# All low parts of the split weights made by VectorE, none by GpSimd

## The chip, the cores and the metric

The kernel runs on one core of one Trainium2 chip, as one launch. The metric is device time in microseconds (us), from the first instruction to the last, with what the launch puts around them. Lower is better. Engines are named as in the profile: PE is TensorE (PEld its weight load), DVE is VectorE, ACT is ScalarE, POOL is GpSimd, SP is the engine that issues the weight DMAs. L905 is line 905 of the kernel.

## The reference

256 tokens of width 1024 go through two stacks of two layers each, all in fp32. The first stack has four token mixers side by side in each layer (retention, a state-space scan, mLSTM, gated linear attention), a gated merge of their outputs, and a feed-forward: a plain one in layer 0, eight experts with top 2 in layer 1. The second stack has a modulation from a vector `c`, sliding-window attention and a feed-forward. Cut to what this change concerns, each mixer layer of the first stack is:

```python
def token_mixers(h, pos, w_in, ..., w_branch, w_out):
    u = h @ w_in                                   # 1024 -> all inputs of the four branches, and mgate (4096 columns)
    (rq, rk, rv, rg, sz, sxbc, sdt, gq, gk, gv, gr, ga,
     mqk, mv, mo, mi, mf, mgate) = _split_cols(u)
    ...                                            # four scans over the tokens, one per branch
    ybr = jnp.stack([y_ret, y_ssd, y_gla, y_ml], axis=2)
    gates = jax.nn.sigmoid(mgate.reshape(bsz, seq, N_BRANCH, D_MODEL))
    merged = jnp.sum(gates * jnp.einsum('bsnv,nvd->bsnd', ybr, w_branch), axis=2)
    return merged @ w_out
```

## The kernel before

**Split products.** A product in fp32 precision is made of three products of a faster format (fp32r). Each operand is written as a high part plus a low part, and TensorE adds high x high, high x low and low x high. The weights come from memory in pieces of 128 x 2048 numbers (1 MB), in a ring `raw` of 5 slots. For each piece, ScalarE makes the high part into `whi` (`split_high`, L899), and then one engine makes the low part into `wlo` as `raw - whi` (`split_low`, L905). `whi` and `wlo` have 3 slots each: ScalarE may write a slot only when TensorE has read the piece that was in it. SP loads a new piece into a slot of `raw` when the low part of the old one is made. The modulation weights (`ada_w`) are used in plain fp32 straight from `raw` and are not split at all.

**Which engine makes the low part.** `piece(name, of, lo_on)` takes `"V"` (VectorE) or `"G"` (GpSimd). `project_tokens` and `two_features` pass it on. In the kernel before, 24 pieces of each mixer layer, 48 in all, are marked `"G"`: retention's values (p0.2, two pieces), the middle piece of the state-space inputs (p1.1), mLSTM's values (p2.2, two), the gated attention's queries and values (p3.0, one, and p3.1, two), and the gates (g0.0 to g3.1, eight steps of two pieces). All other pieces are on VectorE.

**The order on each engine.** Each engine runs a list of steps. The order of the steps of a mixer layer is written out by hand in `MIXER`; steps such as `ret1`, `ssd4`, `gla5` are pieces of the scans and stand between the projections, so that TensorE has products to do while the vector work of a scan runs. Every step runs on TensorE, ScalarE and VectorE, each doing its own share of it. The splits are not in the list. They are put in by `wait_ge` and `split`: TensorE notes at each piece that it will need the two pieces after it as well (`AHEAD`), and when another engine is about to wait for a result of TensorE, it first makes its own share of all the pieces that TensorE had asked for by then:

```python
            if self.split_piece is not None and not self.splitting:
                self.reach = max(self.reach, self.board.need.get(key, 0))
                self.split()
```

So a low part on VectorE stands in the middle of the scan's vector work, at a place that this rule decides, and everything behind it on VectorE waits until its high part is there. A low part on GpSimd stands in a queue that holds little else: only the inverse roots of the norms (`inverse_root`, L1936 and L1938).

**Names in the rows.** L1460, L1466: small row operations of the mixers on 4 partitions (`rows3`, `rows4`). L568: the transposes `tokcol` that need them. L1359: taps of the causal convolution, with L1024 its tanh on ScalarE. L1496, L1498, L1500: rotary of the queries and keys (`ret1`), L491 and L492 the scores. L1383, L1384, L1035: decays of a scan. L1391, L1393, L1936, L1938, L1398: a head norm, over VectorE, GpSimd and VectorE again. L1413, L1417: merge of a gated branch. L1601 to L1605, L524, L1426: a level of the gated attention (`gla`): factors, scores, and the copy that frees the four PSUM banks of the level before. L410: any group of matmuls that add into one bank.

Of the kernel before, what the change touches and what calls it, by code (L numbers as in the profile page):

```python
# [14 lines left out]
P = 128  # L15
# [29 lines left out]
COLS = {}  # L45
# [131 lines left out]
def program(nc, a, out):  # L177
    with ExitStack() as ctx:
# [79 lines left out]
        rv, rg, rqk, rot_raw = carve(0, NT * MIX, NT * MIX, 4 * T, 4 * T)  # L258
        pad1, conv1, sz, xs, xdt = carve(1, 6 * (T + PAD), 6 * T, NT * MIX, NT * MIX, NT * MIX)
        mva, mo, pad2, conv2 = carve(2, NT * NH * (HD + 1), NT * MIX, 4 * (T + PAD), 4 * T)  # L260
        gv, gr, glaq, glak, glaG, glaE, glaX0, glaX1 = carve(3, NT * MIX, NT * MIX, *[T] * 6)
# [143 lines left out]
        def tensor_program(t):  # L405
# [62 lines left out]
            def two_features(name, w, c0, stage, lo_on="V"):  # L468
                read, parts = piece(name, full_piece(w, c0), lo_on)
                bank = t.take(name)  # L470
                for j in range(2):
                    m = project_features(full(parts), j * P, stage, bank, j * T)
                t.then_inc(m, ("full", name), read)
# [55 lines left out]
            def mixer_step(l, step):  # L529
                w, here = a["w_in"][l], (l, "mix")  # L530
                kind, _, n = step.partition(".")
                if step == "z":
                    read, parts = piece(("z", l), strips_piece(w, [(COLS[z], 32) for z in ("sdt", "ga", "mi", "mf")]))
                    bank = t.take(("z", l))
                    t.then_inc(project_features(full(parts, P), 0, here, bank, 0), ("full", ("z", l)), read)
                elif step == "alpha":
                    bank = t.take(("alpha", l))
                    t.wait_ge(("gate_feat", l))
                    at = COLUMN[("w_alpha", l)]
                    t.then_inc(group(bank[:, 0:T], [(cols[0:16, at:at + P], gate_feat[0:16, :])]), ("full", ("alpha", l)))  # L540
                elif step in ("p0.0", "p0.1"):
                    two_features(("p0", l, int(n)), w, COLS["rq" if n == "0" else "rk"], here)
                elif step == "p0.2":
                    project_tokens(("p0v", l), w, COLS["rv"], here, "G")
                elif kind == "p1" and n < "3":
                    two_features(("p1", l, int(n)), w, COLS["sxbc"] + int(n) * 2 * P, here, "G" if n == "1" else "V")
                elif step == "p1.3":
                    read, parts = piece(("p1z", l), full_piece(w, COLS["sz"]))
                    wf = full(parts)
                    for tt in range(NT):  # L550
                        bank = t.take(("p1z", l, tt))
                        m = product(bank[:, 0:MIX], [(stat_tokens(k, tt), (wf[0][:, k, :], wf[1][:, k, :])) for k in range(KD)])
                        t.then_inc(m, ("full", ("p1z", l, tt)), *([read] if tt else []))
                elif kind == "p2" and n < "2":
                    two_features(("p2", l, int(n)), w, COLS["mqk"] + int(n) * 2 * P, here)
                elif step == "p2.2":
                    project_tokens(("p2v", l), w, COLS["mv"], here, "G")
                elif step == "p3.0":
                    two_features(("p3", l), w, COLS["gq"], here, "G")
                elif step == "p3.1":  # L560
                    project_tokens(("p3v", l), w, COLS["gv"], here, "G")
                elif step == "tokcol":
                    t.wait_ge(("rows", l))
                    bank = t.take(("tokcol", l))
                    for i, r_ in enumerate((ACS, DT, CJ, TMP2)):
                        for tt in range(NT):
                            c = (i * NT + tt) * NH
                            m = transpose(bank[:, c:c + NH], row(r_)[:, pick_tokens(tt)], ident[0:NH, 0:NH])  # L568
                    t.then_inc(m, ("full", ("tokcol", l)))
                elif kind[0] == "d":  # L570
                    for z in mod_chunks["branch", 0][2 * int(kind[1:]):2 * int(kind[1:]) + 2]:
                        modulation_piece(*z)
                elif kind[0] == "g" and kind[1] != "l":
                    project_tokens(("g", l, int(kind[1]), int(n)), w, COLS["mgate"] + branch_order[int(kind[1])] * D + int(n) * BANK,
                                   here, "G")
                elif kind[0] == "a":
                    merge(l, int(kind[1]))
                elif kind[:3] == "ret":
                    retention(l, int(kind[3:]))
                elif kind[:3] == "ssd":  # L580
                    ssd(l, int(kind[3:]))
                elif kind[:2] == "ml":
                    mlstm(l, int(kind[2:]))
                elif kind[:3] == "gla":
                    gla(l, int(kind[3:]))
# [1603 lines left out]
```

## Time and profile before

| | us |
|---|---|
| time, median of 3 runs (lowest to highest) | 2478.57 (2476.72 to 2479.82) |
| the profiled execution, its time | 2476.41 |
| its span from first to last instruction | 2474.5 |
| PE busy in it | 2160.6 (87%) |
| DVE busy | 1543.9 (62%) |
| ACT busy | 1197.2 (48%) |
| POOL busy | 287.6 (12%) |

The profiled execution is 2.2 us below the median of the timed runs, and its time is 1.9 us longer than its span. Busy time is summed over an engine's instructions; matmuls overlap. An engine that is busy for 12% of the span can still hold up another one, so the table alone does not say what a change to it is worth. The two mixer layers of the first stack lie at about 20 to 400 us and 604 to 945 us; the experts of layer 1 follow until about 1800 us.

### The profile page before, as it was taken

How to read it: one execution, taken by the hardware profiler on the slowest of the kernel's cores; microseconds unless marked ns; L12 is line 12 of the kernel's file. 1: busy time of each engine (PE TensorE's matmuls, PEld its weight loads, DVE VectorE, ACT ScalarE, POOL GpSimd, SP SyncE). 2: the span in 40 equal slices, each digit the busy share in tenths (PEclk: the TensorE clock that was granted, in tenths of full speed). 3: DMA queues.
4: the chain of work that ended last, by engine and by line, in shares of the span. 5: the costliest groups of instructions: out<-in, count | busy, mean ns of one | idle time of the engine just before them, and what ended most of it. 6: DMA issues, size and time to landing. Idle time of an engine off the chain costs nothing.

```text
span 2474.5 us, 25557 instructions
## 1 busy us (share of the span) xinstructions
PE 2160.6 (87%) x10570; PEld 1769.1 (71%) x10570; DVE 1543.9 (62%) x1538; ACT 1197.2 (48%) x1251; POOL 287.6 (12%) x135
## 2 busy tenths in 40 slices
PE   6788778998889766999999999999967799787997
PEld 5676556886777654778787787877856488676886
DVE  2664454544456652788888888888855444554444
ACT  5443224443634322776676676766733344333442
POOL 2354400000337400000000000000000100100000
PEclk9888889998989888999999999999988799988999
DMA  8354556556434336799999999999961666523551
GB/s 260 103 190 168 187 191 235 189 184 193 135 119 153 119 117 237 263 353 330 341 345 339 360 325 338 366 341 345 362 219 59 230 205 197 189 85 96 189 189 54
DMA packets 369319, 550.49 MB, mean 222 GB/s; under 512 B 21030, under 2 KB 295078, under 8 KB 362150
## 3 DMA queue, kind: packets, MB, share of 16 engines
q1 hardware_dynamic: 365168, 534.82, 64.3%
q10 hardware_dynamic: 4028, 13.95, 1.5%
q8 instruction: 86, 1.41, 0.2%
q14 instruction: 37, 0.30, 0.0%
HBM read 547.58 MB, written 1.15 MB: 222 GB/s over the span
## 4 chain that ended last, share of the span: by engine, by line
PE 78%; DVE 10%; ACT 5%; DMA 2%; POOL 2%; issue 1%; ACTq 0%; SPq 0%; DVEq 0%; POOLq 0%
PE bank L410 74%; PE bank L436 2%; DVE wlo L905 2%; ACT whi L899 2%; POOL wlo L905 1%; DVE arena L1359 1%; POOL small L1938 1%; PE bank L485 1%; DVE arena L1500 1%; DMA raw<-in_moe_w 1%; DVE xn L1417 0%; DVE scoresB L1426 0%; ACT xn L964 0%; DVE arena L1498 0%; DMA xn<-in_lmask 0%
## 5 line engine op out<-in xcount | busy, mean ns | idle before, releaser
L905 DVE TENSOR_TENSOR wlo<-raw,whi 128x2048 fp32r<-128x2048 f32 (+1 forms) x413 | 944.2, 2290 | 403.7 <-ACT whi L899 403.6
L899 ACT ACTIVATE whi<-raw 128x2048 fp32r<-128x2048 f32 (+1 forms) x461 | 878.5, 1908 | 429.9 <-PE bank L410 374.1
L410 PE MATMUL bank<-whi,hThi 128*128 128x512 f32 (+2 forms) x1104 | 444.7, 403 | 41.5 <-POOL wlo L905 20.2
L410 PE MATMUL bank<-wlo,hThi 128*128 128x512 f32 (+2 forms) x1104 | 434.6, 394 | 0.0
L410 PE MATMUL bank<-whi,hTlo 128*128 128x512 f32 (+2 forms) x1104 | 434.0, 393 | 0.0
L410 PE MATMUL bank<-whi,slots_hi 128*128 128x512 f32 x704 | 283.8, 403 | 1.9 <-DVE slots_lo L1714 1.9
L410 PEld LDWEIGHTS bank<-whi,hThi 128*128 128x128 f32 x1104 | 217.1, 197 | 89.3 <-POOL wlo L905 21.7
L410 PE MATMUL bank<-whi,slots_lo 128*128 128x512 f32 x704 | 277.8, 395 | 0.0
L410 PE MATMUL bank<-wlo,slots_hi 128*128 128x512 f32 x704 | 277.8, 395 | 0.0
L905 POOL TENSOR_TENSOR wlo<-raw,whi 128x2048 fp32r<-128x2048 f32 x48 | 227.3, 4752 | 248.9 <-ACT whi L899 248.8
L410 PEld LDWEIGHTS bank<-whi,hTlo 128*128 128x128 f32 x1104 | 215.7, 195 | 44.2
L410 PEld LDWEIGHTS bank<-wlo,hThi 128*128 128x128 f32 x1104 | 217.0, 197 | 42.1 <-issue 0.9
L1936 POOL TENSOR_SCALAR small<-small 128x1 f32<-128x1 f32 (+2 forms) x34 | 13.9, 409 | 1310.9 <-ACT xn L964 1174.3
L410 PEld LDWEIGHTS bank<-whi,slots_hi 128*128 128x128 f32 x704 | 134.9, 192 | 28.5 <-issue 2.1
L410 PEld LDWEIGHTS bank<-whi,slots_lo 128*128 128x128 f32 x704 | 134.0, 190 | 29.0
L410 PEld LDWEIGHTS bank<-wlo,slots_hi 128*128 128x128 f32 x704 | 135.1, 192 | 26.6
L410 PE MATMUL bank<-whi,gatedThi_moe_sparse 128*128 128x512 f32 x352 | 137.7, 391 | 3.1 <-DVE gatedTlo_moe_sparse L1649 3.1
L410 PE MATMUL bank<-whi,gatedTlo_moe_sparse 128*128 128x512 f32 x352 | 138.0, 392 | 0.0
L410 PE MATMUL bank<-wlo,gatedThi_moe_sparse 128*128 128x512 f32 x352 | 137.6, 391 | 0.0
L410 PE MATMUL bank<-hThi,whi 128*128 128x256 f32 x352 | 108.1, 307 | 19.8 <-DVE wlo L905 7.0
L410 PE MATMUL bank<-whi,gatedThi_ffn 128*128 128x512 f32 x264 | 104.0, 394 | 9.0 <-DVE gatedTlo_ffn L1649 9.0
L410 PE MATMUL bank<-hTlo,whi 128*128 128x256 f32 x352 | 105.5, 300 | 0.0
(290 smaller groups left out, 2633.4 us busy)
## 6 DMA issues: line engine op xcount, KB each, us to landing
raw<-in_moe_w SPq DMA_DIRECT2D x352, 512.0 KB, 5.8
raw<-in_moe_w SPq DMA_DIRECT2D x88, 1024.0 KB, 7.4
raw<-in_w_in SPq DMA_DIRECT2D x72, 1024.0 KB, 5.1
raw<-in_ada_w SPq DMA_DIRECT2D x48, 1024.0 KB, 5.0
raw<-in_ffn_w SPq DMA_DIRECT2D x44, 512.0 KB, 4.9
raw<-in_w_gate SPq DMA_DIRECT2D x44, 512.0 KB, 4.0
raw<-in_w_up SPq DMA_DIRECT2D x44, 512.0 KB, 5.0
raw<-in_w_down SPq DMA_DIRECT2D x22, 1024.0 KB, 4.9
```

Source lines behind the costliest of these rows:

```text
L410: m = mm(dst, l_, r_, start=start and i == 0, stop=stop and i == len(pairs) - 1)
L436: m = transpose(bank[:, j * P:(j + 1) * P], block, ident)
L485: m = mm(bank[32 * j:32 * j + 32, :], cc[:, k:k + 1].broadcast_to([P, 32]), w[:, half_of(j)], start=k == 0, stop=k == KD - 1, tile_positio ...
L899: s.then_inc(s.unit.activation(split_slot(whi, p)[:, 0:n], slot_of_ring(raw, p, NRAW)[:, 0:n], ACT.Copy), ("hi", p), sem="weights_hi")
L905: e.then_inc(e.unit.tensor_tensor(split_slot(wlo, p)[:, 0:n], slot_of_ring(raw, p, NRAW)[:, 0:n], split_slot(whi, p)[:, 0:n].bitcast(F32), ...
L1359: v.then_inc(stt(conv3[:, c, :], pad3[:, c, k:k + T], col(name + "_w", l, k * n + c), conv3[:, c, :], ALU.mult, ALU.add), *([(name + "_sum ...
L1500: v.then_inc(tensor(out3[:, two, :], out3[:, two, :], raw3[:, two, :], ALU.add), ("rotated", l, i))
L1936: g.then_inc(scalar(dst, sums, 1.0 / n, EPS, ALU.mult, ALU.add))
L1938: g.then_inc(tensor(dst, dst, const("power").broadcast_to(list(dst.shape)), ALU.pow), name)
```

## The change

Seven places pass `"V"` where they passed `"G"` (for p1 the condition falls away). `split_low_on_gpsimd` stays and has nothing to do.

```diff
                 elif step == "p0.2":
-                    project_tokens(("p0v", l), w, COLS["rv"], here, "G")
+                    project_tokens(("p0v", l), w, COLS["rv"], here, "V")
                 elif kind == "p1" and n < "3":
-                    two_features(("p1", l, int(n)), w, COLS["sxbc"] + int(n) * 2 * P, here, "G" if n == "1" else "V")
+                    two_features(("p1", l, int(n)), w, COLS["sxbc"] + int(n) * 2 * P, here, "V")
...
                 elif step == "p2.2":
-                    project_tokens(("p2v", l), w, COLS["mv"], here, "G")
+                    project_tokens(("p2v", l), w, COLS["mv"], here, "V")
                 elif step == "p3.0":
-                    two_features(("p3", l), w, COLS["gq"], here, "G")
+                    two_features(("p3", l), w, COLS["gq"], here, "V")
                 elif step == "p3.1":
-                    project_tokens(("p3v", l), w, COLS["gv"], here, "G")
+                    project_tokens(("p3v", l), w, COLS["gv"], here, "V")
...
                     project_tokens(("g", l, int(kind[1]), int(n)), w, COLS["mgate"] + branch_order[int(kind[1])] * D + int(n) * BANK,
-                                   here, "G")
+                                   here, "V")
```

The instructions of PE, ACT and SP stand in the same order as before. POOL loses its 48 L905. On DVE they stand where the rule above puts them. The first place is in layer 0, from the row sums of the mixers to retention's scores (names as above). The two low parts added in the first piece are those of g0.0.

```order
 L1460 TENSOR_TENSOR rowbuf<-rowbuf 4x256
 L1462 SCALAR_TENSOR_TENSOR rowbuf<-cst,rowbuf 4x256
+L905 TENSOR_TENSOR wlo<-raw,whi 128x2048
 L1359 SCALAR_TENSOR_TENSOR arena<-arena,cols 128x256 x6
 L1364 SCALAR_TENSOR_TENSOR arena<-arena 128x256 x2
 L1465 TENSOR_SCALAR rowbuf<-rowbuf 4x256
 L1466 TENSOR_TENSOR rowbuf<-rowbuf 4x256
+L905 TENSOR_TENSOR wlo<-raw,whi 128x2048
 L1349 SCALAR_TENSOR_TENSOR arena<-arena,bank 128x256 x2
```

One of the two now stands ahead of the work that TensorE's `tokcol` waits for (L1466), the other behind it.

The second place is in layer 0, in the gated attention. Between the factors of its sixth level (32x4) and the copy L1426 that frees banks, DVE before has nothing; with the change it makes both low parts of g3.0 there, and both of g3.1 one level later.

```order
+L1604 TENSOR_TENSOR arena<-arena 128x32x4
+L1605 TENSOR_TENSOR arena<-arena 128x32x4
+L905 TENSOR_TENSOR wlo<-raw,whi 128x2048 x2
+L1426 COPY_PREDICATED scoresB<-lmask,bank 128x2x128 x4
+L1601 TENSOR_TENSOR arena<-arena 128x64x2
+L1602 TENSOR_TENSOR arena<-arena 128x64x2
+L905 TENSOR_TENSOR wlo<-raw,whi 128x2048 x2
+L1604 TENSOR_TENSOR arena<-arena 128x64x2
```

All of these rows carry a +, since the comparison takes the whole stretch as one block; against the kernel before, only the two rows of L905 are new in it. They put the level's bank-freeing copy behind two low parts.

The third place is in layer 1, after the head norm of mLSTM, whose last step is L1398 (rows of the changed kernel, then of the kernel before).

```order
L1398 TENSOR_TENSOR obuf<-obuf,small 128x512
L905 TENSOR_TENSOR wlo<-raw,whi 128x2048 x4
L1402 SCALAR_TENSOR_TENSOR ylo<-bank,yhi 128x512
L905 TENSOR_TENSOR wlo<-raw,whi 128x2048
L1413 SCALAR_TENSOR_TENSOR gate_tanh<-gate_tanh,bank 128x512 x4
```

```order
L1398 TENSOR_TENSOR obuf<-obuf,small 128x512
L905 TENSOR_TENSOR wlo<-raw,whi 128x2048
L1402 SCALAR_TENSOR_TENSOR ylo<-bank,yhi 128x512
L1413 SCALAR_TENSOR_TENSOR gate_tanh<-gate_tanh,bank 128x512 x4
```

Three low parts come in ahead of L1402, and one more (the second piece of g3.0) between L1402 and the merge L1413.

## Rows read from the trace of the kernel before

**Rows 1.** The page: busy time of each engine, and its costliest group.

```profile
PE 2160.6 (87%) x10570; PEld 1769.1 (71%) x10570; DVE 1543.9 (62%) x1538; ACT 1197.2 (48%) x1251; POOL 287.6 (12%) x135
...
L905 DVE TENSOR_TENSOR wlo<-raw,whi 128x2048 fp32r<-128x2048 f32 (+1 forms) x413 | 944.2, 2290 | 403.7 <-ACT whi L899 403.6
```

**Rows 2.** Two mixer layers: busy of PE, PEld, DVE, ACT, POOL; clock, DMA share, GB/s.

```profile
20.00:400.00 380.00, 308.52 (x1729) 246.88 (x1727) 196.54 (x293) 142.32 (x186) 123.19 (x36) 0.90 0.52 177
604.00:945.00 341.00, 278.84 (x1528) 236.01 (x1529) 191.26 (x274) 129.90 (x158) 121.33 (x32) 0.87 0.42 139
```

**Rows 3.** Low parts on POOL: ns min/median/max, first and last start; waits for them.

```profile
L905 POOL TENSOR_TENSOR wlo<-raw,whi x48: 4501/4606/6097, 34.9 to 862.9; 128x2048 fp32r<-128x2048 f32 x48
...
PE bank L410 <- POOL wlo L905: 23.5, 5, 7.9
```

**Rows 4.** DVE in order of time, layer 0: start, us, instruction, [idle before].

```profile
80.91 4.62 DVE L1460 TENSOR_TENSOR rowbuf<-rowbuf 4x256 f32<-4x256 f32 x1
...
86.17 2.43 DVE L1359 SCALAR_TENSOR_TENSOR arena<-arena,cols 128x256 f32<-128x256 f32 x6
...
89.75 0.40 DVE L1466 TENSOR_TENSOR rowbuf<-rowbuf 4x256 f32<-4x256 f32 x1
...
97.64 4.98 DVE L1500 TENSOR_TENSOR arena<-arena 128x512 f32<-128x512 f32 x1
...
107.97 0.69 DVE L1500 TENSOR_TENSOR arena<-arena 128x512 f32<-128x512 f32 x1
```

**Rows 5.** PE in order of time, tokcol and retention's scores, both layers.

```profile
90.65 1.01 PE L568 MATMUL bank<-cst,rowbuf 4*128 4x4 f32 x8 [6.58 <-ACT rowbuf L1065]
...
108.71 1.23 PE L491 MATMUL bank<-arena 64*128 64x256 f32 x4 [2.56 <-DVE arena L1500]
...
676.82 1.01 PE L568 MATMUL bank<-cst,rowbuf 4*128 4x4 f32 x8 [7.66 <-ACT rowbuf L1065]
...
695.01 0.49 PE L491 MATMUL bank<-arena 64*128 64x256 f32 x2 [2.28 <-DVE arena L1500]
```

**Rows 6.** PE in order of time: four first matmuls that waited for POOL.

```profile
168.25 0.79 PE L410 MATMUL bank<-whi,hThi 128*128 128x512 f32 x1 [3.78 <-POOL wlo L905]
...
208.48 0.58 PE L410 MATMUL bank<-hThi,whi 128*128 128x256 f32 x1 [3.32 <-POOL wlo L905]
...
242.16 0.79 PE L410 MATMUL bank<-whi,hThi 128*128 128x512 f32 x1 [7.87 <-POOL wlo L905]
...
750.41 0.80 PE L410 MATMUL bank<-whi,hThi 128*128 128x512 f32 x1 [3.83 <-POOL wlo L905]
```

**Rows 7.** DVE in order of time: end of mLSTM's head norm, layer 0.

```profile
237.68 4.98 DVE L1398 TENSOR_TENSOR obuf<-obuf,small 128x512 f32<-128x512 f32 x1 [1.81 <-POOL small L1938]
```

**Rows 8.** Layer 1, in order of time: a convolution on DVE, high parts on ACT.

```profile
733.81 5.75 DVE L1359 SCALAR_TENSOR_TENSOR arena<-arena,cols 128x256 f32<-128x256 f32 x6 [2.98 <-ACT arena L1020]
...
743.87 3.69 ACT L899 ACTIVATE whi<-raw 128x2048 fp32r<-128x2048 f32 x2
```

**Rows 9.** Gated attention, layer 0, in order of time: ACT, DVE, PE.

```profile
289.25 5.49 ACT L899 ACTIVATE whi<-raw 128x2048 fp32r<-128x2048 f32 x3
...
289.78 1.43 DVE L1426 COPY_PREDICATED scoresB<-lmask,bank 128x256 f32<-128x256 uint8 x4
...
290.37 0.73 PE L524 MATMUL bank<-arena 32*128 32x128 f32 x16 [1.98 <-DVE scoresB L1426]
295.82 0.80 PE L410 MATMUL bank<-whi,hThi 128*128 128x512 f32 x1 [4.72 <-POOL wlo L905]
```

**Rows 10.** Layer 1, ahead of the gated attention: high part on ACT, last merge on DVE.

```profile
828.75 1.92 ACT L899 ACTIVATE whi<-raw 128x2048 fp32r<-128x2048 f32 x1
...
833.72 0.69 DVE L1413 SCALAR_TENSOR_TENSOR gate_tanh<-gate_tanh,bank 128x512 f32<-128x512 f32 x1 [0.69 <-PE bank L410]
```

**Rows 11.** Two stretches behind waits of Rows 6; columns as in Rows 2.

```profile
168.00:172.00 4.00, 3.75 (x9) 2.97 (x10) 3.90 (x3) 0.00 (x0) 4.00 (x2) 0.50 0.96 338
208.00:217.00 9.00, 8.52 (x48) 8.40 (x48) 2.04 (x1) 1.70 (x1) 9.00 (x3) 0.64 0.60 199
```

## The prediction

> **What bounds the kernel now.** I read the page first. TensorE is busy 87% of the span and VectorE 62%; a low part takes VectorE 2.29 us [rows 1]. Then the view of GpSimd's low parts: 48 of them, 4.5 us at the least, 4.6 at the median, all between 35 and 868 us, all of them in the two mixer layers [rows 3]. The windows of these two layers show VectorE at 197 of 380 us and 191 of 341 us, about half, and GpSimd at 123 and 121 us [rows 2]. The view of waits gives the first figure that matters: matmuls waited five times for a GpSimd low part, 23.5 us in all [rows 3]. The last view, VectorE in order of time, gives the second. The row operation L1460 takes 4.62 us, and L1466 on as many elements takes 0.40. L1500 takes 4.98 us and, ten microseconds later, 0.69 [rows 4]. The long ones are those under which a GpSimd low part ran. So GpSimd costs twice: by its own slowness where TensorE waits for it, and by holding up VectorE in the stretches where VectorE is what TensorE waits for.
>
> **What the change removes and adds.** 48 low parts leave GpSimd; VectorE gets 48 x 2.29 = 110 us more work. With about 190 us per layer it goes to some 250 less what its stalls give back: still below 75% of either layer. So I go by place: where does TensorE wait, and what ends the wait.
>
> *Retention, layer 0.* Before L1466 one stall goes (L1460, 4.62 - 0.40 = 4.22) and one low part comes in (2.29), so the row sums end 1.93 us earlier. TensorE's tokcol, idle for 6.58 us before them [rows 5], starts that much earlier. Behind it VectorE does the rotary, where three operations were stalled, the longest by 4.98 - 0.69 = 4.3 us [rows 4]; against one low part that comes in ahead of them, even this one stall alone makes the rotary end earlier by 2 us more, and the three together by far more than TensorE can use. TensorE can use only the 2.56 us for which it was idle before the scores [rows 5], since its g0.0 products lie in between. Gain 1.93 + 2.56 = 4.5.
>
> *Retention, layer 1.* The same instructions and the same kind of stall: 1.93, and the idle time before the scores is 2.28 [rows 5]. Gain 4.2.
>
> *First low part of g1.0, layer 0* (TensorE waits 3.78 until 168.25) and *of p3.0* (3.32 until 208.48) [rows 6]. VectorE is free at both places when the high part is done, so 4.5 becomes 2.29. Gain 2.2 each. At p3.0, VectorE makes a second low part before the decays L1383; it is hidden under the p3.0 products, and would cost up to 2.3 us if these did not cover it.
>
> *g2.0, layer 0* (7.87 until 242.16) [rows 6]. GpSimd's low part stands behind its own inverse root there, and both it and VectorE's L1398 (at 237.68, 4.98 us, stalled) set out when that root is done [rows 7]. On VectorE the low part stands behind L1398: 237.68 + 0.69 + 2.29 = 240.66. Gain 1.5.
>
> *g1.0, layer 1* (3.83 until 750.41) [rows 6]. Its high part is made at 743.87, right behind the decays' exponentials, which hang on the convolution that starts at 733.81 and takes 5.75 us for six taps [rows 8]. Six taps without a stall took 2.43 us [rows 4]. One low part (2.29) now stands ahead of them, but VectorE was idle for 2.98 us there [rows 8], which takes in about half of it: the low part ends, I estimate, 1.2 us after the taps could have begun. So they end 3.32 - 1.2 = 2.1 us earlier, and the high part with them; the low part then takes 2.29 instead of 4.5. Together 4.3, more than the wait. Gain 3.8, the whole of it.
>
> *Gated attention, layer 0: a loss.* Both low parts of g3.0 now stand between the factors of a level and the copy L1426 that frees the banks, for which TensorE's next level already waits [rows 9]. Their high parts are made from 289.25, three in 5.49 us [rows 9]: the first is done at 291.1. VectorE then works until 291.1 + 2 x 2.29 = 295.7, the first copy (1.43 / 4) ends at 296.1, the level takes 0.73, and g3.0 starts at 296.9 instead of 295.82. Loss 1.1 instead of a gain of 2.2.
>
> *Gated attention, layer 1: a loss.* One low part stands ahead of the merge L1413. Its high part is done at 830.7 (828.75 + 1.92), the low part at 833.0, four merges of 0.69 at 835.8; before, the last ended at 834.4 [rows 10]. Loss 1.4.
>
> *At nothing:* the other low parts. Of the 24 in a layer, most are made while TensorE has products of 5 to 6 us per piece in front of it (48 matmuls took 8.52 us even at a low clock [rows 11], two pieces of VectorE 4.6). If this cover is gone, each costs up to 2.29. GpSimd's remaining roots are not queued behind anything any more. The experts and the second stack are left as they are.
>
> **Sum of the places:** 4.5 + 4.2 + 2.2 + 2.2 + 1.5 + 3.8 - 1.1 - 1.4 = 15.9 us.
>
> **The lock, by row and by rule.** The rows show no sharing: a 0.40 us operation lasts as long as the GpSimd instruction that it met (4.62) [rows 4]. The Trainium skill, "SBUF — State Buffer", section "Who interferes with whom", says that VectorE instructions with two SBUF inputs take an exclusive lock against a GpSimd instruction that reads SBUF, and the second to start blocks fully. By this rule as by the row, the stall goes with its cause. Were it bandwidth that is shared, a doubled 0.40 would be 0.80, L1460 would give back 0.4 and retention would lose 1.9 us per layer at tokcol in place of gaining it, a sum of about 8; no row speaks for that.
>
> **The clock.** Behind two of the waits TensorE ran at a granted clock of 0.50 for 4 us and 0.64 for 9 us [rows 11]; its levels are 1.2 and 2.4 GHz, so that is 2.0 + 3.2 = 5.2 us lost to the lower one. What came before was an idle TensorE. With those waits shorter some of it comes back: bounds 0 and 5.2, and I take 3, since the wait at p3.0 falls to 1.1 us and that at g1.0 to 1.6. The Trainium skill, "TensorE: Matmul & The Clock Gate", Part 1, says that activity releases the throttle. By it the gain is at the upper end if these places stay active; the rows do not show at what wait that begins.
>
> **Forecast.** 15.9 + 3 = 18.9. The profiled execution took 2476.41, so 2457.5; the median stands 2.2 higher, so 2459.7.
>
> **Rivals.**
> *TensorE takes more of the idle time back.* The whole clock term (5.2), the same again at the other waits that shrink (three more places, up to 1.7 each), and no loss in the gated attention (2.5): 15.9 + 5.2 + 5.1 + 2.5 = 29, time about 2450. For it: every stretch behind a wait that I looked at was slow. Against it: the clock also falls at waits that stay. Chance 0.16.
>
> *No change: the waits come back elsewhere.* Where VectorE's stalls go, ScalarE's high parts and the head norms may be next, each within a microsecond or two behind. If only the three pure waits for GpSimd (2.2 + 2.2 + 1.5) count and the two losses and a low part at each tokcol (2 x 2.3 = 4.6) eat them, the sum is -1.2: 2480. For it: in retention three engines take turns, so a gain can vanish there. Against it: the idle time before tokcol names L1065 and through it VectorE alone. Chance 0.08.
>
> *Slower: VectorE is held by waits for high parts.* A low part on VectorE must wait for its high part, and that one for TensorE to read an older piece. If it stands ahead of something for which TensorE waits, the two turn into a ring in which nothing overlaps. The gated attention of layer 0 is such a place. Should a high part come a whole piece later there and in the merges of layer 1 (5.75 us of products each), six such holds give 34.5 us, less 18.9: 2478.6 + 15.6 = 2494. It decides from the fourth hold on (18.9 / 5.75 = 3.3). Against it: in the rows the high parts are done before or within 1.5 us of when VectorE gets to them. The Trainium skill, "Perfetto Trace Analysis", section "Optimizing Scalar/DVE Operations", gives a reason of its own: work between these two engines shares a port, so moving it might not help, and offloading VectorE pays when it is saturated. By it the change would undo a useful offload; the trace does not agree, with VectorE at half of either layer. Chance 0.06.
>
> **How the numbers follow.** My forecast, with a gain of 8 to 27 us, has 0.70. The range reaches from the first rival's time to where half of the places fail: 2450 to 2471. It leaves 0.2 outside. About 0.2% (5 us) is what a measurement can tell from no change. Faster than 2473.6: 0.87; within 0.2%: 0.07; slower than 2483.5: 0.06.
>
> **What would show it.** L1460, L1498, L1500 and L1398 in the changed trace near 0.4 to 0.7 us; no L905 on GpSimd; tokcol's wait in layer 0 near 4.6 us; no wait before retention's scores; g1.0's first matmul in layer 1 right behind L492; level six of the gated attention in layer 0 waiting some 7 us for L1426. Wrong would make me: stalls of the small VectorE operations that stay without GpSimd, or L905 on VectorE with idle time of 3 us and more before it in front of a waiting TensorE.

## The result, and the profile after

The changed kernel takes 2449.49 us (median of 4 runs, 2448.74 to 2450.9), the kernel before 2478.07 beside it (4 runs, 2476.72 to 2479.82). The ratio is 0.9885, 95% interval 0.9868 to 0.9902: 28.6 us faster. I had forecast 2459.7, a gain of 18.9; direction right, size too small by ten, and the result lies half a microsecond outside the range. The profiled execution took 2448.74, its span is 2446.9. One run of a later experiment, g0_and_waits, took 2883.18 us at a mean granted clock of 0.727 and is left out of its median.

The page of the changed kernel, busy times and costliest group, answers to [rows 1]:

```profile
PE 2150.1 (88%) x10570; PEld 1760.5 (72%) x10570; DVE 1561.0 (64%) x1586; ACT 1196.8 (49%) x1251; POOL 60.4 (2%) x87
...
L905 DVE TENSOR_TENSOR wlo<-raw,whi 128x2048 fp32r<-128x2048 f32 (+1 forms) x461 | 1052.3, 2287 | 442.9 <-ACT whi L899 442.3
```

VectorE made 48 low parts more, 108.1 us, and its busy time rose by 17.1: 91 us came back from stalls. The next thing to look at is TensorE's own entry. The same 10570 instructions are busy for 2150.1 instead of 2160.6 us. So the 27.6 us by which the span fell are two things: 10.5 us less busy time, and 17.1 us less idle time (2474.5 - 2160.6 = 313.9 before, 296.8 now). The windows of the two mixer layers, the same work as in [rows 2], say where:

```profile
20.00:384.00 364.00, 301.00 (x1728) 240.46 (x1726) 205.92 (x317) 142.50 (x186) 9.39 (x12) 0.91 0.53 185
588.00:918.50 330.50, 276.64 (x1528) 234.94 (x1529) 198.86 (x299) 129.68 (x158) 7.88 (x8) 0.89 0.43 143
```

Layer 0 takes 16.0 us less, of which 7.5 are busy time; layer 1 takes 10.5 less, of which 2.2 are busy time. The view of waits, matmuls by what they waited for:

```profile
PE bank L410 <- DVE wlo L905: 31.4, 10, 6.3
```

The line for POOL's low parts (23.5 us, [rows 3]) is gone; VectorE's own line rose from 22.6 to 31.4. VectorE in order of time, layer 0, against [rows 4]:

```profile
81.31 0.41 DVE L1460 TENSOR_TENSOR rowbuf<-rowbuf 4x256 f32<-4x256 f32 x1
...
82.36 2.25 DVE L905 TENSOR_TENSOR wlo<-raw,whi 128x2048 fp32r<-128x2048 f32 x1
...
95.25 0.69 DVE L1500 TENSOR_TENSOR arena<-arena 128x512 f32<-128x512 f32 x1
```

L1460 fell from 4.62 to 0.41 and L1500 from 4.98 to 0.69, with the new low part between. TensorE in order of time, the places of [rows 5, 6, 9]:

```profile
89.06 1.01 PE L568 MATMUL bank<-cst,rowbuf 4*128 4x4 f32 x8 [5.75 <-ACT rowbuf L1065]
...
160.81 0.50 PE L410 MATMUL bank<-whi,hThi 128*128 128x512 f32 x1 [1.51 <-DVE wlo L905]
...
196.34 0.39 PE L410 MATMUL bank<-hThi,whi 128*128 128x256 f32 x1 [1.04 <-DVE wlo L905]
...
225.88 0.79 PE L410 MATMUL bank<-whi,hThi 128*128 128x512 f32 x1 [6.34 <-DVE wlo L905]
...
280.22 1.24 PE L524 MATMUL bank<-arena 32*128 32x128 f32 x16 [7.84 <-DVE scoresB L1426]
281.39 0.80 PE L410 MATMUL bank<-whi,hThi 128*128 128x512 f32 x1
...
723.69 0.48 PE L410 MATMUL bank<-whi,hThi 128*128 128x512 f32 x1
```

Each wait can be set beside its forecast; and beside it stands what the 48 products behind it took (one step of a projection), from the start of the first to the end of the last, which I had hardly looked at:

| place | idle before, after | gain | forecast | block behind, before, after |
|---|---|---|---|---|
| tokcol, scores, layer 0 | 6.58 + 2.56, 5.75 + 0 | 3.4 | 4.5 | 11.76, 13.05 (g0.0) |
| g1.0, layer 0 | 3.78, 1.51 | 2.3 | 2.2 | 13.60, 11.18 |
| p3.0 | 3.32, 1.04 | 2.3 | 2.2 | 8.61, 6.00 |
| g2.0 | 7.87, 6.34 | 1.5 | 1.5 | 12.55, 12.72 |
| gated attention, layer 0 | 1.98 + 4.72, 7.84 | -1.1 | -1.1 | 13.01, 12.29 |
| tokcol, scores, layer 1 | 7.66 + 2.28, 5.61 + 0 | 4.3 | 4.2 | 12.18, 11.56 (g0.0) |
| g1.0, layer 1 | 3.83, 0 | 3.8 | 3.8 | 12.74, 11.16 |
| level zero, layer 1 | 7.04, 7.26 | -0.2 | -1.4 | |
| sum | | 16.3 | 15.9 | |

The blocks of the table are 6.5 us shorter together, of the 10.5 that TensorE's busy time lost, and not each of them: g0.0 in layer 0 took 1.3 us longer behind a shorter wait.

The windows over p3.0's products, here behind a wait of 1.04 us; [rows 11] has them behind 3.32:

```profile
196.34:202.35 6.01, 6.01 (x50) 5.88 (x50) 5.10 (x10) 2.08 (x3) 0.00 (x0) 1.00 1.01 405
```

The granted clock is 1.00, thus 2.4 GHz throughout, where it was 0.64: products that the change doesn't touch are 2.6 us shorter. The experiments ask three things: whether GpSimd's reads held VectorE up; what the clock behind the waits is worth; and whether the parts add up. Lines of their profiles are shifted by a few numbers where code was added ahead (L1466 is then the L1460 of before).

### The profile page after: what moved, and what is told of

It is laid out like the page before. It is cut to its first block, busy times and chain, and to the rows that moved or that the text cites. A ratio compares the mean times of both kernels' runs of the same rounds, so it can differ in the third digit from the quotient of the medians.

```text
span 2446.9 us, 25557 instructions
## 1 busy us (share of the span) xinstructions
PE 2150.1 (88%) x10570; PEld 1760.5 (72%) x10570; DVE 1561.0 (64%) x1586; ACT 1196.8 (49%) x1251; POOL 60.4 (2%) x87
## 4 chain that ended last, share of the span: by engine, by line
PE 80%; DVE 9%; ACT 5%; DMA 3%; issue 1%; POOL 1%; ACTq 0%; SPq 0%; DVEq 0%; POOLq 0%
PE bank L410 76%; DVE wlo L905 3%; PE bank L436 2%; ACT whi L899 2%; DMA raw<-in_moe_w 1%; POOL small L1938 1%; PE bank L485 1%; DVE scoresB L1426 1%; ACT xn L964 1%; DVE arena L1359 0%; DVE xn L1417 0%; DMA raw<-in_ada_w 0%; DMA xn<-in_lmask 0%; DVE outputs_lo L1731 0%; POOL small L1936 0%
## 5 line engine op out<-in xcount | busy, mean ns | idle before, releaser
L905 DVE TENSOR_TENSOR wlo<-raw,whi 128x2048 fp32r<-128x2048 f32 (+1 forms) x461 | 1052.3, 2287 | 442.9 <-ACT whi L899 442.3
L410 PE MATMUL bank<-hThi,wlo 128*128 128x256 f32 x352 | 104.5, 297 | 0.0
L410 PE MATMUL bank<-wlo,gatedThi_ffn 128*128 128x512 f32 x264 | 103.8, 393 | 0.0
```

Of the source, the lines that this page charges most:

```text
L410: m = mm(dst, l_, r_, start=start and i == 0, stop=stop and i == len(pairs) - 1)
L905: e.then_inc(e.unit.tensor_tensor(split_slot(wlo, p)[:, 0:n], slot_of_ring(raw, p, NRAW)[:, 0:n], split_slot(whi, p)[:, 0:n].bitcast(F32), ...
```

## Does GpSimd hold VectorE up, apart from being slow?

**g0_only.** The kernel before, with only g0.0's and g0.1's low parts on VectorE. TensorE waits for none of these by name.

```diff
-                                   here, "G")
+                                   here, "V" if kind == "g0" else "G")
```

> Only the gate pieces g0.0 and g0.1 of both layers (8 low parts) go to VectorE, the other 40 stay on GpSimd. Theory A (VectorE's small operations were held by GpSimd's low parts, and retention was waiting for them): L1460, L1498 and L1500 fall from 4.6 to 5.0 us to 0.4 to 0.7, tokcol starts 1.6 to 2 us earlier, the wait before the scores goes, 8.7 us in both layers, and 1 to 3 us more by the clock: 2466 to 2469. Rival (GpSimd is only slow, and retention's gain in the changed kernel comes from p1.1 and p0.2 being on VectorE): no change, 2478.

Measured 2467.57 (6 runs; before 2476.96), ratio 0.9959 (0.9943 to 0.9975): 9.4 us from eight low parts that nobody waited for, as the stall theory had it. Its span has 9.1 us less idle time of TensorE (304.8) and 1.4 more busy time (2162.0): all of this gain is waiting, and the 1 to 3 us that I expected from the clock did not come.

**lock.** The changed kernel, where GpSimd reads SBUF at its former times and nothing uses the result.

```diff
+            if was_on_gpsimd(plan[p][0]) and plan[p][0][1] == 0:
+                g.wait_ge(("hi", p))
+                for free in (cs_, sn_, cs_, sn_):
+                    g.own()
+                    g.then_inc(g.unit.tensor_tensor(free.bitcast(mybir.dt.bfloat16), cst[:, 0:2 * T], cst[:, 0:2 * T], ALU.subtract))
```

> The changed kernel; in layer 0 GpSimd also makes four subtractions of 512 columns for each of its former low parts, set off by the same high part, which read constants and whose result nothing uses. So GpSimd reads SBUF at the former times, about as long, but no low part comes from it. Theory A (GpSimd held VectorE up, apart from being slow): VectorE's small operations in layer 0 last up to the length of one such subtraction (1 to 1.5 us) again, and its low parts too; some of what layer 0 gained is lost: 3 to 8 us slower than the changed kernel, 2452 to 2458. Rival (only GpSimd's slowness where TensorE waited for it mattered): nothing is waited for, 2449.5 as without the subtractions.

Measured 2467.32 (12 runs; before 2476.22), ratio 0.9967 (0.9956 to 0.9979): some 18 us lost, where 3 to 8 were expected. VectorE and GpSimd in order of time:

```profile
81.37 1.08 DVE L1466 TENSOR_TENSOR rowbuf<-rowbuf 4x256 f32<-4x256 f32 x1
82.48 1.41 DVE L1468 TENSOR_TENSOR_SCAN rowbuf<-cst,rowbuf 4x256 f32<-4x256 f32 x1
83.82 2.25 DVE L905 TENSOR_TENSOR wlo<-raw,whi 128x2048 fp32r<-128x2048 f32 x1
...
173.45 6.06 DVE L905 TENSOR_TENSOR wlo<-raw,whi 128x2048 fp32r<-128x2048 f32 x2
```
```profile
82.25 1.10 POOL L921 TENSOR_TENSOR rope_sin<-cst 128x512 bf16<-128x512 f32 x1
83.43 3.94 POOL L921 TENSOR_TENSOR rope_cos<-cst 128x512 bf16<-128x512 f32 x1
```

The row operation takes 1.08 where it took 0.41, and GpSimd's subtraction, else 1.1 us, lasts 3.94 where it meets VectorE's scan and then its low part at 83.82, which itself lasts 2.25 as ever: each engine can hold the other. Two low parts at 173.45 take 6.06 us where they would take 4.5. But these subtractions also stood ahead of GpSimd's inverse roots, so the run mixes two causes. The next takes them apart.

**no_read.** The same, with memsets, which write SBUF and read nothing.

```diff
-                for free in (cs_, sn_, cs_, sn_):
+                for free in 4 * (cs_, sn_):
...
-                    g.then_inc(g.unit.tensor_tensor(free.bitcast(mybir.dt.bfloat16), cst[:, 0:2 * T], cst[:, 0:2 * T], ALU.subtract))
+                    g.then_inc(g.unit.memset(free.bitcast(mybir.dt.bfloat16), 0.0))
```

> The changed kernel; in layer 0 GpSimd makes eight memsets of 512 columns for each of its former low parts, set off by the same high part, in place of the four subtractions of constants that made it 2467. They queue ahead of GpSimd's inverse roots as those did, but read nothing from SBUF. Theory A (VectorE is held up while GpSimd reads SBUF): VectorE's small operations and low parts in layer 0 last as in the changed kernel (0.41, 2.25), and the time is within 3 us of 2449.5, as far as the roots are not late. Rival (what cost 17 us was the queue ahead of the roots, or GpSimd being busy at all): 2460 to 2467 again.

Measured 2451.47 (4 runs; before 2476.47), ratio 0.9894 (0.9879 to 0.9909), the changed kernel within the error. GpSimd and VectorE in order of time:

```profile
80.05 0.52 POOL L921 MEMSET rope_cos<- 128x512 bf16 x1 [25.25 <-ACT whi L899]
80.64 0.52 POOL L921 MEMSET rope_sin<- 128x512 bf16 x1
```
```profile
80.67 0.41 DVE L1466 TENSOR_TENSOR rowbuf<-rowbuf 4x256 f32<-4x256 f32 x1
```

GpSimd has about as much work as the 96 subtractions would be if nothing held them (192 memsets, 100.8 us, against 96 x 1.1; in lock they took 159.5), queued in the same places, and L1466 takes 0.41 beside a running memset. So GpSimd being busy, and queued ahead of its roots, did not by itself cost the 18 us. What stops VectorE is a GpSimd instruction that reads SBUF; the two instructions differ in kind as well, and that the reading alone does it is inferred.

## What is the clock behind the waits worth?

**before_busy.** No wait is shortened; TensorE works through four of its five waits for GpSimd (the fifth, before g3.0, stays as it is).

```diff
+            def keep_busy(bank, n):
+                for _ in range(n):
+                    mm(bank[:, :], hi3[:, 0, 0:P], hThi[:, 0:BANK], start=True, stop=True)
...
+                        first = t.take((name, 0))
+                        keep_busy(first, idle)
...
```

> The kernel before, with all 48 low parts on GpSimd, and TensorE doing extra products of 512 columns (15, 15, 12 and 32 of them, overwritten by the real ones) while it waits for the low parts of g1.0 (both layers), p3.0 and g2.0. They add computation that the kernel does not need and leave the waits as long as they were. Theory A (what the changed kernel gained beyond the waits is the clock, which falls when TensorE idles): the products behind take 11.2, 6.0 and 11.2 us instead of 13.6, 8.6 and 12.7, some 6.6 us in all and perhaps 1 at g2.0: about 2471. Theory B (not the clock): no gain, 2478, or a little more where the extra products run over.

Measured 2469.9 (10 runs; before 2476.96), ratio 0.9966 (0.9956 to 0.9975): 7.1 us gained by more work. TensorE at p3.0, then the window over its products:

```profile
203.45 4.31 PE L450 MATMUL bank<-hThi 128*128 128x512 f32 x12
207.55 0.42 PE L410 MATMUL bank<-hThi,whi 128*128 128x256 f32 x1
```
```profile
207.50:213.80 6.30, 6.30 (x51) 6.11 (x49) 0.97 (x1) 0.57 (x1) 6.30 (x2) 0.94 0.51 173
```

The wait is no shorter (4.0 us from the last instruction before it, now nearly all filled). The products start 0.9 us earlier than in the kernel before and end 3.3 earlier. The granted clock behind a wait is a price of its own, and here it can be bought off.

**twice.** The changed kernel, with the first low parts of g1.0 (both layers), g2.0 and p3.0 made twice on VectorE.

```diff
+                if plan[p][0] in slow_names and plan[p - 1][0] != plan[p][0]:
...
+                    v.then_inc(v.unit.tensor_tensor(split_slot(wlo, p)[:, 0:n], slot_of_ring(raw, p, NRAW)[:, 0:n],
+                                                    split_slot(whi, p)[:, 0:n].bitcast(F32), ALU.subtract))
```

> The changed kernel, with the low part made twice in a row on VectorE for four pieces (first of g1.0 in both layers, of p3.0 and of g2.0 in layer 0), so that TensorE waits for VectorE about as long as it waited for GpSimd, and nothing runs on GpSimd. 2.3 us more at three places and 1.8 at g1.0 of layer 1, 8.6 in all. Theory A (waits bring the lower clock with them): another 4 to 6 us, 2462 to 2464. Theory B (the clock does not depend on these waits): 2458.

Measured 2466.07 (8 runs; before 2476.96), ratio 0.9952 (0.9938 to 0.9966): 16.6 us lost. TensorE at p3.0, and the window over its products:

```profile
201.46 0.58 PE L410 MATMUL bank<-hThi,whi 128*128 128x256 f32 x1 [3.37 <-DVE wlo L905]
```
```profile
201.40:209.90 8.50, 8.44 (x50) 8.31 (x52) 7.47 (x12) 3.52 (x4) 0.00 (x0) 0.68 0.78 277
```

With 3.4 us of wait back, the clock is back at 0.68, without GpSimd having anything to do with it. The span is 16.7 us longer (2463.6): 6.5 of it are idle time, and 10.2 are TensorE's busy time, back at 2160.3. Not all of the 10.2 belongs to the waits. Three of them came back, with 7.0 us (p3.0 3.37, g1.0 of layer 0 3.84, g2.0 8.66); at g1.0 of layer 1 TensorE still doesn't wait. The blocks behind the three take 2.4, 1.6 and 0.9 us more (8.38, 12.79 and 13.66), 4.9 together. Much of the rest stands at two blocks of layer 1 ahead of which no wait came back: g0.0 takes 13.09 instead of 11.56, and a block ahead of g1.0 12.81 instead of 11.18. shift_after, the next run, has none of these waits back and the same two blocks at 13.07 and 12.82. So 7.0 us of wait cost 4.9 more by the clock behind them, or 3.4 if p3.0 is set against the 7.5 us that it takes in shift_after behind the short wait.

**shift_after, shift_after2, shift_before.** A row operation of 0.28 us is made 4 or 8 times more ahead of tokcol in layer 0, so that what hangs on it comes 1.1 or 2.2 us later.

```diff
+                    for _ in range(4 if l == 0 else 0):
+                        v.then_inc(scalar(row(NM), row(MX), -1.0, None, ALU.mult))
+                        v.own()
```

(8 in place of 4 in shift_after2; shift_before has the 4 in the kernel before.)

> The changed kernel, with the 0.28 us row operation L1465 made four more times in layer 0, ahead of the row sums for which tokcol waits: everything behind it comes about 1.1 us later, nothing else is different. If each wait and each block costs what it costs wherever it falls, the kernel takes 1.1 us more: 2450.6. If the granted clock behind the waits depends on when they come, the time goes up or down by more: the blocks that differed between the kernel before and the changed one at places with equal waits (up to 2.8 us each) would move it by 1 to 4 us either way, 2447 to 2454.

> The changed kernel, with that row operation made eight more times, about 2.2 us later. If four more had cost 4.7 us by chance of where the waits fell, this need not cost twice as much: anything from 2449 to 2457, with the same blocks as there (p3.0 at 6.0 or 7.5 us; the blocks behind tokcol and behind the decays in layer 1 at 11.2 to 11.6 or 12.8 to 13.1) at one or the other length. If the delay itself were paid about fourfold: 2449.5 + 9.4 = 2459.

> The kernel before, with the row operation L1465 made four more times in layer 0, about 1.1 us later at tokcol and all that follows. If the price of the clock behind waits does not depend on when they come: 2477 + 1.1 = 2478. If it does, as in the changed kernel, where the same delay cost 4.7 us: 2473 to 2483, and then the gain of the change, measured between two single placements in time, carries an uncertainty of some 3 us that no repetition of the same kernel takes away.

Measured: shift_after 2454.23 (5 runs; before 2476.22), ratio 0.9903 (0.9884 to 0.9921); shift_after2 2452.97 (5 runs; before 2474.6), 0.9917 (0.9903 to 0.993); shift_before 2477.85 (11 runs; before 2474.6), 1.0007 (0.9995 to 1.0019). In the changed kernel 1.1 us of delay cost 4.7 and 2.2 us cost 3.5 by the medians, 4.5 and 7.9 by the ratios. At p3.0 of shift_after, TensorE and the window:

```profile
195.54 0.39 PE L410 MATMUL bank<-hThi,whi 128*128 128x256 f32 x1 [1.04 <-DVE wlo L905]
```
```profile
195.50:203.10 7.60, 7.56 (x50) 7.43 (x52) 6.57 (x11) 3.54 (x4) 0.00 (x0) 0.78 1.02 400
```

The wait is the same 1.04 us to the hundredth, and the 50 products take 7.5 us instead of 6.0. So what the clock takes behind a wait depends not on its length alone. It doesn't hang on the delay alone either. Ahead of the added operations stands a block of 48 products behind a wait of 3.67 us; the windows over it, in shift_after and in the changed kernel:

```profile
75.42:83.89 8.47, 8.47 (x48) 8.27 (x48) 8.24 (x16) 4.81 (x8) 0.00 (x0) 0.67 0.38 126
```
```profile
75.97:83.31 7.34, 7.34 (x48) 7.14 (x48) 7.11 (x16) 4.81 (x8) 0.00 (x0) 0.79 0.43 145
```

Here 1.1 us differ before the delay has begun. Runs of one program differ too: shift_after took 2449.79 to 2456.14, waits_only (below) 2466.9 to 2479.17. By the medians the changed kernel as it stands would be favoured by 1.3 to 3.6 us (2452.97 - 2.2 and 2454.23 - 1.1, less 2449.49); that is an estimate, for the interval of shift_after overlaps that of the changed kernel, 0.9868 to 0.9902. With the delay of 1.1 in both kernels the ratios give 0.9903 / 1.0007, a gain of 1.0%, 26 us: the gain itself stays.

**g30.** One low part less between the factors and level six of the gated attention. (`"VG"` puts a step's first piece on VectorE and its second on GpSimd, by a small change of `project_tokens` that isn't shown.)

```diff
-                                   here, "V")
+                                   here, "VG" if (kind, n) == ("g3", "0") else "V")
```

> The changed kernel, with the second low part of g3.0 back on GpSimd in both layers. In layer 0 VectorE then has one low part less between the factors and the copies for which TensorE's level six waits (7.84 us). Theory A (the loss in the gated attention is VectorE's low parts standing ahead of the copies): the wait falls by 2.3 and the time by about 2 us, unless the low part on GpSimd meets the copies themselves, which then last up to 4.5 us. So 2447 if it gets past them, 2450 or more if it meets them. Rival (the wait is set by the level's own factors): no change, 2449.5.

Measured 2451.28 (4 runs; before 2476.22), ratio 0.9897 (0.9878 to 0.9917). TensorE at level six, and the window over p3.0, 77 us ahead of the edit:

```profile
278.81 1.23 PE L524 MATMUL bank<-arena 32*128 32x128 f32 x16 [5.64 <-DVE scoresB L1426]
```
```profile
194.80:202.40 7.60, 7.55 (x50) 7.42 (x52) 6.57 (x11) 3.53 (x4) 0.00 (x0) 0.78 1.02 402
```

The wait fell from 7.84 to 5.64 as expected, and the time did not: busy time is 4.7 us higher (2154.8), partly at places that the edit can't have changed. The 2.1 us by which idle time fell (294.7) are less than what the clock's share differs by from one program to the next.

**after_busy, before_all_busy, shift_after_busy, more_busy.** Both kernels with products that nothing reads in the waits at tokcol, at two head norms a layer and at the g's and p3.0; then the delay of 1.1 in the changed one; then g30 and the second stack's long waits as well.

```diff
-                    t.wait_ge(("rows", l))
                     bank = t.take(("tokcol", l))
+                    keep_busy(bank, 22)
+                    t.wait_ge(("rows", l))
...
```

> The changed kernel, in which TensorE runs products of 512 columns that nothing reads (12 to 32 of them, 0.22 us each) while it waits at tokcol and at the head norms of the first and the last branch in both layers, and 6, 4 and 26 at g1.0, p3.0 and g2.0 of layer 0. No wait gets shorter and nothing else moves. Theory A (a wait of TensorE is paid twice: once by itself and once by the lower clock of the products behind it): the slow blocks that are left behind these waits (the products behind tokcol in layer 0, 13.05 where 11.2 is possible; behind the first head norm, 8.3 for 6; behind the last one, 7.6 and 7.3 for 6) get fast, 3 to 8 us less than the changed kernel's 2449.5: 2442 to 2446. Theory B (the ten microseconds beyond the idle time came from something else than the clock): no change or the time of the dummies where they overrun, 2449 to 2452.

> The kernel before (48 low parts on GpSimd), with products that nothing reads while TensorE waits at tokcol and at the first and last head norms in both layers, at g1.0 of both layers, at p3.0 and at g2.0: the waits that the changed kernel had filled at 2432 us, and those for GpSimd's low parts. With TensorE active on both sides of the comparison the clock has little part in it. Theory A (the change is worth the idle time that I summed by place, 16.4 us in the two traces, and the rest of its 28.6 us is the clock behind waits): about 2432 + 16.4 = 2448, at most 2451. Rival (the change saves 26 to 28 us of something else than waits and clock): 2432 + 27 = 2459.

> The version with filled waits (2432 us), with the row operation made four more times in layer 0, 1.1 us later. Theory A (the dependence on timing comes from the clock behind idle waits, and with those filled it is mostly gone): 2432 + 1.1, thus 2432 to 2434. Rival (the places where blocks are long or short by chance are not those waits): 2432 plus or minus 4 us, as the same delay cost 4.7 in the changed kernel.

> The changed kernel with its waits filled as in the 2432 us version, and three things more: the second low part of g3.0 on GpSimd (it cut level six's wait by 2.2 us, which the clock took back), products at the wait for level zero of the gated attention in both layers, and 32 to 54 products while the second stack's mixers and feed forwards wait 8 to 14 us for their modulated input. Theory A: the 2.2 us stay now, and the transposes and first products behind the four long waits get faster (4.95 to 3.5 us each, and what is behind them): 5 to 9 us less than 2432, 2423 to 2427. Rival (long waits' clock loss is not saved by activity ahead, since these products end before the wait does): 2430.

Measured: after_busy 2431.99 (5 runs; before 2476.22), ratio 0.9824 (0.9805 to 0.9843); before_all_busy 2460.95 (5 runs; before 2474.6), 0.9942 (0.9928 to 0.9956); shift_after_busy 2439.75 (5 runs; before 2476.47), 0.9844 (0.9831 to 0.9857); more_busy 2431.07 (5 runs; before 2474.6), 0.9824 (0.9807 to 0.9841). Filling the waits is worth another 15 to 17.5 us to the changed kernel, more than the 3 to 8 that I expected, but three of my expectations fell. shift_after_busy is not within 1.1 us: it is slower by 7.8 by the medians and 5 by the ratios. That the delay did this is not shown, for the two intervals overlap, and the five runs of after_busy itself fall in two groups, 2430.36 to 2431.99 and 2439.03 to 2439.64; what it does show is that filled waits don't make the time steady. more_busy was to take 2423 to 2427 and took 0.9 less than after_busy, which is nothing: with all four long waits of the second stack filled as well, and g30's edit in, the rival's 2430 came. And the difference between the two filled kernels is 29 us, not 16 to 19. The trace of before_all_busy shows one reason. TensorE and GpSimd at g1.0 of before_all_busy:

```profile
166.44 0.50 PE L410 MATMUL bank<-whi,hThi 128*128 128x512 f32 x1 [2.07 <-POOL wlo L919]
```
```profile
161.05 10.62 POOL L919 TENSOR_TENSOR wlo<-raw,whi 128x2048 fp32r<-128x2048 f32 x2 [9.63 <-ACT whi L913]
```

3.66 us of filling and then 2.07 of idle time are 5.7 where the wait was 3.78: TensorE came 3.5 us earlier, by a higher clock in the blocks ahead, and GpSimd's pair of low parts only 2.6, now 5.3 us each. In the kernel before a faster TensorE waits longer at such a place; in after_busy it goes through this one without a wait. That part of the gain is neither a wait of the trace of before nor a clock behind it, and the forecast had no place for it. How the rest of the 29 divides stays open.

## Do the parts add up?

**waits_only, g0_and_waits.** The kernel before, with the low parts of four first pieces on VectorE: g1.0's in both layers, g2.0's and the only one of p3.0 in layer 0; then with the second pieces of these and g0 as well, 15 in all (the expectation says 14, a miscount).

```diff
+                                   here, "VG" if (l, kind, n) in ((0, "g1", "0"), (1, "g1", "0"), (0, "g2", "0")) else "G")
...
```

> Only four low parts go from GpSimd to VectorE: the first piece of g1.0 in both layers, of p3.0 in layer 0 and of g2.0 in layer 0, each of which TensorE waited for. Both theories expect the waits to shrink by 2.2, 2.2, 1.5 and 2.3 us, 8.2 in all. Theory A (a shorter wait also gives back the clock behind it): the products behind the waits of g1.0 (13.6 us before), p3.0 (8.6) and g1.0 of layer 1 (12.7) come to 11.2, 6.0 and 11.2 as in the changed kernel, 6.6 us more, so 14.8 below the kernel before, about 2463. Theory B (the extra speed of the changed kernel comes from elsewhere, such as the lighter load on GpSimd): 8.2 below, about 2470.

> The kernel before, with the low parts of g0.0 and g0.1 (both layers), g1.0 (both layers), p3.0 and g2.0 (layer 0) on VectorE, whole, 14 of the 48; the others stay on GpSimd. Theory A (all of the gain is at these places): 16 us of idle time and about 7 of clock, 2477 - 23 = 2454, or less by what the gated attention doesn't lose here. Rival (the low parts left on GpSimd meet VectorE's at these very places, as in the version with only the four first pieces, where one took 6.58 us at g2.0): 2460 to 2467.

Measured: waits_only 2476.55 (10 runs, 2466.9 to 2479.17; before 2476.96), ratio 0.9999 (0.9989 to 1.0009); g0_and_waits 2461.81 (6 runs, 2456.76 to 2467.17; before 2476.47), 0.9936 (0.992 to 0.9951). The waits that were for GpSimd, moved by themselves, gave nothing, where both theories expected 8 us or more: in the trace the idle time of TensorE is 314.5 us, before it was 313.9. At g2.0 of waits_only (profiled in the fastest of its runs, 2466.9), VectorE, GpSimd and TensorE:

```profile
229.46 4.98 DVE L1398 TENSOR_TENSOR obuf<-obuf,small 128x512 f32<-128x512 f32 x1 [1.81 <-POOL small L1938]
234.37 6.58 DVE L905 TENSOR_TENSOR wlo<-raw,whi 128x2048 fp32r<-128x2048 f32 x1
```
```profile
229.40 9.40 POOL L905 TENSOR_TENSOR wlo<-raw,whi 128x2048 fp32r<-128x2048 f32 x2
```
```profile
241.00 0.80 PE L410 MATMUL bank<-whi,hThi 128*128 128x512 f32 x1 [14.93 <-DVE wlo L905]
```

The next two low parts, still GpSimd's, run from the same moment; VectorE's multiply lasts 4.98 and its low part 6.58, and TensorE waits 14.93 us where it waited 7.87: these 7.1 us eat what the other three places gave. A low part left on GpSimd beside one on VectorE is here worse than both on GpSimd. With 15 of the 48 moved, 15 to 16 us came (by the medians and by the ratio), within the rival's 2460 to 2467 and about half of the change; g0 alone had given 9 to 10 of them. There is no trace of g0_and_waits at the usual clock, so where it lost the rest is not shown.

## Why the prediction came out as it did

- **Where TensorE waits: right.** 16.3 us measured against a sum of 15.9. g1.0 in both layers, p3.0, g2.0 and the loss of 1.1 at level six came within 0.1 us. Retention in layer 0 gave up 3.4 us of idle time for 4.5: the wait before the scores went, and tokcol started 1.6 earlier (1.93; 2.0 if counted from L1457, which starts at 79.61 before and 80.01 after), but TensorE's idle time there fell by 0.8 only, since the block ahead of it was done 0.8 earlier too. The loss of 1.4 in layer 1 was 0.2: the merges came 1.0 us later beside TensorE's products, and L1417 behind them fell from 3.04 to 2.29, a stall by GpSimd that I had not counted. So the sum is as close as it is in part by luck, since these two differences of over 1 us cancel.
- **The stall as a lock: right,** shown by lock against no_read, and by g0_only; the stalled rows came to 0.41 and 0.69 as forecast.
- **The clock: the step that failed.** The term of the sum that was mis-sized is the clock's: I took 3 us, between bounds of 0 and 5.2 worked out from two waits, and put the clock everywhere else at nothing. Measured are 10.5 us less busy time. At the two places of the bounds, g1.0 and p3.0 of layer 0, the blocks are 2.4 and 2.6 us shorter, so the upper bound was about right and my 3 too low. The other 5.5 stand at places that I never looked at, such as g1.0 of layer 1 (1.6) and p2.2 of layer 0, from 12.83 to 11.17. That waits make the clock fall is shown: 7.1 us gained by filling four, 3.4 to 4.9 lost at the three that came back in twice. What is not settled is how much of the 10.5 is the change's own. Of p3.0's 2.6 us, 1.5 are there in the changed kernel and no_read, and not in five other versions with the same wait; and the block ahead of tokcol took 8.52 before and 7.34 after, with nothing changed up to there.
- **The rivals.** The first, in which TensorE takes back more (2450), is what happened, though not quite by its working: it took the losses in the gated attention as nothing, and one of them came. The two others did not occur; at no place of the table did a wait for a low part grow.
- **The range.** Its lower end was this rival's time and not below it; had the clock been let double the 15.9, it would have reached to about 2447. And "a gain of 8 to 27 us" is not this range, which is a gain of 7.6 to 28.6; the result lies outside both.

## What to carry to other kernels

Cost a wait of TensorE twice: by its idle time, and by the block behind it, whose busy time at the granted clock (here 8.5 against 6.0 us) stands in the windows; take every block that follows a wait that changes, not two. Where GpSimd and VectorE both work on SBUF operands, an instruction on the slower one is paid for by both, and moving some of them can be worth nothing where moving all is worth 28 us. Where a gain is below some 5 us, run the same kernel with a delay of a microsecond or two before believing it, and each of them several times: the four runs of the changed kernel lay within 2.2 us, neighbours of it that differ by a small delay had medians 3.5 to 4.7 us above, and other versions spread over 9 to 12 us from run to run.

## What the runs showed of the hardware

- GpSimd's subtraction of 512 columns took 1.1 us and, beside a VectorE low part, 3.94; a memset (0.52) neither held VectorE nor was held. The Trainium skill, "SBUF — State Buffer", section "Who interferes with whom", has this lock for VectorE instructions with two SBUF inputs against GpSimd's reads, in both directions. The traces agree on who holds whom. Who came first does not explain every row: the subtraction that lasted 3.94 set out at 83.43, ahead of the low part at 83.82, though with a scan of VectorE's still running, and it was the one held.
- Behind the same wait of 1.04 us the same products of p3.0 ran at a granted clock of 1.00 (6.0 us) in the changed kernel and no_read, and took 7.5 us in shift_after, shift_after2, g30, lock and waits_only (0.78 where shown); behind 3.3 us it was 0.64 to 0.68 (8.4 to 8.6). Eleven programs with the same 10570 TensorE instructions had 2150.1 to 2162.0 us of busy time, each in one profiled execution. What decides between them at an equal wait is not settled here.
- Products that nothing reads, run while TensorE would have waited, took 15 to 17.5 us off the changed kernel (by the ratios and by the medians): 2431.99, the fastest version together with more_busy.
